# Sixteen modulation units beside the first two projection sections, K products in the ring slot, unit loads ahead of x, a maximum in the setup

## What is computed

```
mod = silu(c) @ w_ada + b_ada             # 9 rows (8 samples, 1 prompt) x 6144, in six parts
h = rms_norm(x, g_norm1) * (1 + sc1) + sh1
q, k, v, f, u, gate_b, gate_c = split(h @ w_in)        # one input projection
# samples: q over 4096 cached keys (paged), decay from cached log forgets, softmax, cached values
# prompt: causal attention of 512 tokens with a forget bias; short convolution beside it
x = x + ga1 * (concat(norm(attention), norm(convolution)) @ w_out)
x = x + ga2 * experts(rms_norm(x, g_norm2) * (1 + sc2) + sh2)   # 2 of 32 experts a token
y = rms_norm(x, g_final) * (1 + scf) + shf             # shf, scf = silu(c) @ w_ada_final + b
```

## Time and profile before

| | us |
|---|---|
| median of 3 runs | 970.69 (969.65 to 978.55) |
| the profiled execution | 973.92 |
| its span, first to last instruction | 972.2 |
| TensorE busy | 763.0 |
| VectorE busy | 499.3 |
| mean granted TensorE clock | 0.894 of full |
| moved by DMA | 319.28 MB, 328 GB/s on average |

### The profile page before, as it was taken

How to read it: one execution, slowest core, us unless ns; L and a number is a source line. 1 busy time by engine, 2 the same in 40 slices (tenths; PEclk the granted TensorE clock), 3 DMA queues, 4 the chain that set the end, 5 groups by cost and what they waited for, 6 DMA issues and landing times.

```text
span 972.2 us, 9885 instructions
## 1 busy us (share of the span) xinstructions
PE 763.0 (78%) x3822; PEld 350.9 (36%) x3822; DVE 499.3 (51%) x565; ACT 145.8 (15%) x333; POOL 276.0 (28%) x251
## 2 busy tenths in 40 slices
PE   5399977999998765658797799838888887778854
PEld 1044422333433211213353344434444444444421
DVE  1169979888999768684833232460111111111128
ACT  2221000201000122111142021201111111110103
POOL 4504435456643335251320000002222222212100
PEclk9689989999999877786799799858999999999967
DMA  8957669999999999999997900439999999999642
GB/s 319 400 195 260 217 216 363 420 417 416 418 422 359 364 387 413 398 420 422 377 369 257 351 22 22 173 132 354 411 411 413 412 410 412 412 412 412 273 190 88
DMA packets 67835, 319.28 MB, mean 328 GB/s; under 512 B 11436, under 2 KB 11464, under 8 KB 42567
## 3 DMA queue, kind: packets, MB, share of 16 engines
q1 hardware_dynamic: 41356, 166.53, 43.7%
q0 software_dynamic: 23936, 147.94, 38.3%
q10 hardware_dynamic: 2508, 4.35, 1.2%
HBM read 307.87 MB, written 15.05 MB: 332 GB/s over the span
## 4 chain that ended last, share of the span: by engine, by line
PE 32%; DMA 30%; DVE 24%; SPq 5%; issue 4%; ACT 2%; POOL 1%; DVEq 0%; POOLq 0%; ACTq 0%
DMA R_w<-in_w_expert_up_dram 10%; DVE R_x L1292 8%; DVE R_cm L1295 8%; PE banks L807 7%; DMA R_kv<-in_cache_v_dram,kv_index 6%; PE banks L683 6%; DMA R_kv<-in_cache_k_dram,kv_index 5%; PE banks L831 4%; DMA R_w<-in_w_in_dram 2%; DMA R_part<-in_cache_v_dram,kv_index 2%; PE banks L415 2%; DMA R_w<-in_w_ada_dram 2%; PE banks L823 1%; DMA R_q<-in_w_out_dram 1%; SPq L2013 1%
## 5 line engine op out<-in xcount | busy, mean ns | idle before, releaser
L1295 DVE TENSOR_REDUCE R_cm<-R_x 128x32 f32<-128x2048 f32 x64 | 146.3, 2286 | 7.0 <-DVE R_x L1292 0.5
L455 PE MATMUL banks<-R_h,R_w 128*128 128x512 f32 x320 | 144.8, 600 | 1.0 <-ACT R_h L956 1.0
L1292 DVE TENSOR_TENSOR R_x<-R_kv,R_part 128x2048 f32<-128x2048 f32 x44 | 100.7, 2288 | 15.0 <-DMA R_kv<-in_cache_k_dram,kv_index 14.1
L1856 POOL DMA_INDIRECT R_kv<-in_cache_k_dram,kv_index x44 | 64.1, 1457 | 151.9 <-DVE R_cm L1295 130.9
L415 PE MATMUL banks<-R_kv,R_cm 128*8 128x512 f32 x352 | 54.4, 698 | 47.9 <-DMA R_kv<-in_cache_v_dram,kv_index 41.4
L1913 POOL DMA_INDIRECT expert_rows_scratch<-R_h,R_part x32 | 32.0, 1001 | 204.8 <-DVE R_h L1720 204.8
L1856 POOL DMA_INDIRECT R_kv<-in_cache_v_dram,kv_index x44 | 70.6, 1604 | 67.3 <-PE banks L415 33.9
L455 PEld LDWEIGHTS banks<-R_h,R_w 128*128 128x128 f32 x320 | 58.7, 190 | 79.8 <-issue 78.6
L1717 DVE COPY R_h<-banks 128x128 f32<-128x128 f32 x32 | 9.3, 292 | 144.7 <-PE banks L823 144.7
L1910 POOL DMA_INDIRECT R_t<-h_scratch,R_part x32 | 31.3, 978 | 128.7 <-DVE R_part L1671 119.2
L1720 DVE TENSOR_SCALAR R_h<-banks,R_part 128x512 f32<-128x512 f32 x32 | 24.0, 751 | 71.6 <-PE banks L831 71.6
(11 more groups left out here) (329 smaller groups left out, 1234.2 us busy)
## 6 DMA issues: line engine op xcount, KB each, us to landing
R_w<-in_w_ada_dram SPq DMA_DIRECT2D x24, 1024.0 KB, 9.5
R_w<-in_w_in_dram SPq DMA_DIRECT2D x12, 1024.0 KB, 16.0
R_w<-in_w_ada_final_dram SPq DMA_DIRECT2D x8, 1024.0 KB, 10.3
R_kv<-in_w_expert_gate_dram SPq DMA_DIRECT2D x8, 1024.0 KB, 18.7
R_kv<-in_w_expert_up_dram SPq DMA_DIRECT2D x8, 1024.0 KB, 22.0
R_kv<-in_w_expert_down_dram SPq DMA_DIRECT2D x8, 1024.0 KB, 19.8
R_q<-in_w_expert_gate_dram SPq DMA_DIRECT2D x8, 1024.0 KB, 19.0
R_q<-in_w_expert_up_dram SPq DMA_DIRECT2D x8, 1024.0 KB, 22.8
```

The source lines that it names most:

```text
L455: last = nc.tensor.matmul(bank[m][:, :], l, r, start=(k == 0), stop=(k == KD - 1))
L1292: V.tensor_tensor(prod[:, :, :], kv_ring[slot][:, :, :], spread(q, [P, CH, HW]), ALU.mult)\
L1295: V.reduce_sum(scores[:, b, s * CH:(s + 1) * CH, :], prod[:, :, :].rearrange("p r (h d) -> p r h d", h=H), AX.X).then_inc(S["k_used"], 2)
L1856: pool.indirect_dma_start(kv_flat[slot], None, k_rows if kind == "k" else v_rows, bass.IndirectOffsetOnAxis(kv_index[:, n:n + 1], 0))\
```

## The change

Four pieces. (1) The 16 units of the second and third quarter of `w_ada` get two buffers of their own (`early_unit`: the place of `prod` in R_x, and a free part of R_cm) and are multiplied beside the 16 column groups of sections 0 and 1, into bank 5. ScalarE copies each quarter out, and VectorE's `modulation_early` runs at K chunk 24. Eight units of `w_ada_final` stay in the loop, in steps 1, 4, 7 and 10. (2) VectorE multiplies a K chunk in its ring slot, and the wait for the reduce before it is gone. (3) Units 8 and 9 are issued ahead of x; the gathers start when unit 9 has landed. (4) GpSimd takes a maximum over partitions of the constant ones at the end of its setup.

```diff
-        prod = view(R_x, 0, [CH, HW])
...
+        early_unit = [view(R_x, 0, [4 * SECS]), view(R_cm, 2088, [4 * SECS])]
...
-        ADA_AT = {w: n for n, w in enumerate((0, 1, 3, 4, 6, 8, 10, 12, 14, 16, 19, 22))}
+        ADA_AT = {w: n for n, w in enumerate((1, 4, 7, 10))}
...
+            def early_unit_product(i):
+
+                q, k = divmod(i, KD)
+                if i == 0:
+                    pe.wait_ge(S["f_taken"], 1)
+                if i == KD:
+                    pe.wait_ge(S["part_ready"], 2)
+                pe.wait_ge(early_loaded[i % 2], 16 * (i // 2 + 1))
+                for j in range(4):
+                    last = nc.tensor.matmul(bank[5][32 * j:32 * j + 32, :], c_t[:, k, :],
+                                            early_unit[i % 2][:, j * SECS:(j + 1) * SECS], start=(k == 0), stop=(k == KD - 1))
+                last.then_inc(S["early_used"], 1)
...
                 if c == 0:
                     pe.wait_ge(S["exp_ready"], b + 1)
+                    if b == 0:
+                        pe.wait_ge(S["part_ready"], 3)
...
             def beside_0(i):
+                early_unit_product(i)
...
             def beside_1(i):
+                early_unit_product(KD + i)
...
+            def early_evac(q):
+                act.wait_ge(S["early_used"], KD * (q + 1))
+                copy(part[q][:, :], bank[5][:, :]).then_inc(S["part_ready"], 1)
...
-            act.wait_ge(S["tail_done"], 1)
+            early_evac(0)
+            act.wait_ge(S["side_turned"], 2)
             copy(tail[:, :, :], bank[6][:, 64:64 + B * H].rearrange("p (b h) -> p b h", b=B))\
                 .then_inc(S["tail_evac"], 1)
...
                 if s == 1:
+                    early_evac(1)
                     soft_samples(0)
...
+            def modulation_early():
+
+                dve.wait_ge(S["part_ready"], 3)
+                dve.wait_ge(S["bands_loaded"], 16 * 10)
+                V.tensor_tensor(part[0][:, :], part[0][:, :], band[0][:, :], ALU.add).then_inc(S["mod_ready"], 1)
+                step(V.tensor_tensor(part[1][:, :], part[1][:, :], band[1][:, :], ALU.add))
+                V.scalar_tensor_tensor(part[1][0:64, :], part[1][0:64, :], 1.0, g_band[0][0:64, :], ALU.add, ALU.mult)\
+                    .then_inc(S["mod_ready"], 1)
...
-                if n:
-                    dve.wait_ge(S["k_used"], 2 * n)
-                V.tensor_tensor(prod[:, :, :], kv_ring[slot][:, :, :], spread(q, [P, CH, HW]), ALU.mult)\
-                    .then_inc(S["k_products"], 1)
+                chunk = kv_ring[slot][:, :, :]
+                V.tensor_tensor(chunk, chunk, spread(q, [P, CH, HW]), ALU.mult).then_inc(S["k_products"], 1)
                 dve.wait_ge(S["k_products"], n + 1)
                 V.reduce_sum(scores[:, b, s * CH:(s + 1) * CH, :],
-                             prod[:, :, :].rearrange("p r (h d) -> p r h d", h=H), AX.X).then_inc(S["k_used"], 2)
+                             kv_ring[slot].rearrange("p r (h d) -> p r h d", h=H), AX.X).then_inc(S["k_used"], 2)
...
+            forget_in(H, T, B, bank[5][0:H, 0:B], 1)
             for n in range(K_EARLY):
                 k_chunk(n)
-                if n == 0:
-                    forget_in(H, T, B, bank[5][0:H, 0:B], 1)
-                    V.memset(bank[5][:, :], 0.0)
+                if n == 24:
+                    modulation_early()
...
             def modulation():
 
                 dve.wait_ge(S["part_ready"], 4)
-                dve.wait_ge(S["bands_loaded"], 16 * 12)
-                V.tensor_tensor(part[0][:, :], part[0][:, :], bands[:, 0, :], ALU.add).then_inc(S["mod_ready"], 1)
...
+                dve.wait_ge(S["bands_loaded"], 16 * 16)
+                step(V.tensor_tensor(part[2][:, :], part[2][:, :], band[2][:, :], ALU.add))
...
+            G.partition_all_reduce(top_all[:, 0, :], ones[:, 0:H], P, RED.max)
...
-            pool.wait_ge(S["unit_used"], 8)
+            pool.wait_ge(unit_loaded[0], 16 * 4)
...
+            def early(i):
+
+                if i == 1:
+                    sp.wait_ge(S["h_psum"], 1 + KD)
+                if i >= 2:
+                    sp.wait_ge(S["early_used"], i - 1)
+                v, lo = quads[1 + i // KD]
+                sp.dma_start(early_unit[i % 2][:, :], v[:, i % KD, lo:lo + QUAD]).then_inc(early_loaded[i % 2], 16)
...
-            for u in range(8):
+            for u in range(10):
                 unit(u)
...
-            for u in range(8, 20):
+            for i in range(6):
+                early(i)
+            unit(11)
...
-            sp.wait_ge(S["unit_used"], 38)
+            sp.wait_ge(S["unit_used"], 14 + KD)
             for j in range(4):
...
+                bias_rows(j, 2)
```

More of the change, by code:

```diff
@@ L186, in build @@
         w_flat = view(R_w, 0, [3, 4 * SECS])
[L187 to L189 removed]
+        early_unit = [view(R_x, 0, [4 * SECS]), view(R_cm, 2088, [4 * SECS])]
+        part = [view(R_part, 1536, [SECS]), view(R_x, 1536, [SECS]), view(R_part, 5120, [SECS])]
+        band = [view(R_x, 0, [SECS]), view(R_x, SECS, [SECS]), view(R_w, 0, [SECS])]
+        g_band = [view(R_x, 2 * SECS, [SECS]), view(R_w, SECS, [SECS])]
         mix_a = view(R_h, 0, [C4, T + B])
@@ L269, in build @@
         unit_loaded = [sem(f"unit_loaded{i}") for i in range(3)]
+        early_loaded = [sem(f"early_loaded{i}") for i in range(2)]
         kv_loaded = [sem(f"kv_loaded{i}") for i in range(RING)]
@@ L1076, in conv_sqrt, with ada_evac @@
                 rsqrt(rt_c[:, 0:n], bank[6][:, 0:n], HD).then_inc(S["cn_sqrt"], 1)
-            def ada_evac(q):
-                act.wait_ge(S["unit_used"], 14 + KD * q)
-                if q == 3:
-                    act.wait_ge(S["qb_ready"], B)
-                copy(part[q - 1][:, :], bank[7][:, :]).then_inc(S["part_ready"], 1)
+            def ada_evac():
+                act.wait_ge(S["unit_used"], 14 + KD)
+                act.wait_ge(S["samp_t"], 3)
+                copy(part[2][:, :], bank[7][:, :]).then_inc(S["part_ready"], 1)
             def soft(u):
@@ L1992, in _ @@
             sp.dma_start(x_a[:, :, :], x_prompt.rearrange("b (t p) d -> (b p) t d", p=P)).then_inc(S["x_loaded"], 16)
+            unit(10)
             sp.dma_start(conv_sample[0, :, 0, :], state_conv[0, :, 1, :]).then_inc(S["outs"], 16)
-            for u in range(8, 20):
+            for i in range(6):
+                early(i)
+            unit(11)
+            sp.dma_start(state_rows[:, :], state_conv.rearrange("l b j c -> (l b j) c")).then_inc(S["wf_loaded"], 16)
+            for i in range(6, 10):
+                early(i)
@@ L1995, in _ @@
+            unit(12)
+            for i in range(10, 14):
+                early(i)
+            unit(13)
+            for i in range(14, 16):
+                early(i)
+            sp.wait_ge(S["early_used"], 2 * KD)
+            for j in range(4):
+                bias_rows(j, 0)
+                bias_rows(j, 1)
+            for j in range(2):
+                gain_rows(j, g_band[0], g_norm2)
+            for u in range(14, 18):
                 unit(u)
-                if u == 11:
-                    sp.wait_ge(S["h_row_ready"], 5)
-                    sp.dma_start(state_rows[:, :], state_conv.rearrange("l b j c -> (l b j) c")).then_inc(S["wf_loaded"], 16)
@@ L2012, in _ @@
+            for j in range(2, 4):
+                gain_rows(j, g_band[1], row(g_final))
             for lo, n, src in ((0, NG, w_router_group), (NG, NE, w_router_expert)):
@@ L2021, in _ @@
             sp.dma_start(wo[:, 6:KD, :], w_out_v[:, 6:KD, :]).then_inc(S["wo_conv_loaded"], 16)
-            for q in range(3):
-                sp.wait_ge(S["mod_ready"], q + 1)
-                for j in range(4):
-                    lo = (4 * q + j) * SECS
-                    sp.dma_start(mod_dram[:, lo:lo + SECS], part[q][32 * j:32 * j + B + 1, :]).then_inc(S["mod_out"], 16)
+            keep_modulation(2)
             sp.wait_ge(S["mod_out"], 16 * 12)
```

66 lines of the change are left out of this document (32 added, 34 removed).

## The result

| | us |
|---|---|
| before, median of 20 runs | 974.52 (968.42 to 978.55) |
| changed kernel, median of 20 runs | 966.96 (958.10 to 973.93) |
| ratio, with its 95% interval | 0.9925 (0.9904 to 0.9945), 7.3 us less |
| profiled executions, span | 972.2 before, 962.6 now |
| forecast | 22.7 us less |

The account below looks back on a forecast made before the run. DMA engines were taken as full from 182 to 300 and in the loop (328 to 481), with VectorE the bound there after the change. Terms +10 - 28 - 5 = -23 us, from 970.7 to 948; 8 in 10 for 924 to 970.

Parts of the forecast that it names:

- The start: Setup: unit 9 lands at about 32, x at 39.5; section 0 starts at 54.4, 6 us earlier (4 to 9).
- Sections 0 and 1: Input projection: 16 slots of 5.3 us, set by unit landings of 9.6; section 1 ends at 144.5 (131 to 164).
- the prediction's own signs of being wrong: Landings over 12 us with TensorE waiting, or granted clock below full, in sections 0 and 1; loop still near 145 us.
- The new waits: Around sections 0 to 2: VectorE waits 8 us for the tail sums' copy, ring stops at 153; both hidden.
- The attention loop: 20 K chunks: 153 us become 125 (109 to 142), VectorE's work plus half its waits, 28 us off.
- K products in the slot: VectorE's K products: no wait for the reduce before, 0.18 us a chunk, 3.6 us in the loop, inside the 125.
- The loop's end: Behind the attention loop: bias-row wait avoided, 4.1 us, and output weights issued sooner, 1 us; together 5 (4 to 7).
- C: Rival: the loop follows its score-to-product chain on a slowed TensorE; only 13 us come off, -8, 963; chance 0.18.
- B: Rival: DMA engines alone decide; 29 us gained, 34 to 40 with the loop's end and router rows, 932; chance 0.17.
- D: Rival: two buffers too few, units land in 14.6 us, the loop starts 50 us late, +17, 988; chance 0.12.
- No change: Whole kernel: time within 1% of before, the rest of C and a little of D; chance 0.18.

Follow-up runs that it names:

- e7: Kernel of e1 with the start as before: x ahead of units 8 and 9, gathers from the eighth used unit on; 950.92 us, ratio 0.9736.
- e1: Changed kernel with each V gather, from V chunk 28 on, one step earlier in the gathers' order; 942.63 us, ratio 0.9662.
- e5: Kernel before, with only the gathers' order of e1 (V a step ahead from chunk 28 on); 963.58 us, ratio 0.9891.
- e2: Changed kernel with the eight modulation units that stay in the loop loaded at a sixteenth of their width; 962.28 us, ratio 0.9857.
- e3: Changed kernel with the four router loads issued at the end, behind the last load of x, instead of mid-loop; 973.13 us, ratio 0.9991.

## Why the prediction was wrong

*The start* was right in kind. The gathers begin at 36.1, where unit 9 was to land at 32; x is there at 41.3 (39.5 was taken), and section 0 starts at 56.87 for 54.4. With the same start code the other runs put it between 52.7 and 61.0, and e7 leaves open how much of it is handed on.

*Sections 0 and 1* ended 4.8 us later than the likeliest value and well inside its bounds, 149.3 for 144.5; 2.5 of that is the later start. The length, 92.4 us for 90, is right in part by luck. The forecast had every slot last as long as half a unit's landing, 5.3 us. But where TensorE ran at full clock a column group and its unit product took 4.6 us, and at 14 of 16 products TensorE's row shows no wait. The rest was two waits, 3.29 and 4.26 us, and a clock below full behind them: eight matmuls of a section took 4.93 and 5.39 us there, elsewhere 3.70, and the granted clock was 0.97 from 60 to 122 and 0.88 from 122 to 150, one of the prediction's own signs of being wrong. The early units' loads, as issues of one line:

```profile
DMA to landing us min/median/max: 5.0/8.9/23.8
```

The Trainium skill's rule (DMA: Bandwidth & Descriptors, "Queues, rings and completion order"), that an engine takes the queues with work in turn, had put this end 5 to 7 us behind 144.5, for a gather queue that is never empty. By its own numbers (two units of 1.05 MB at half of 417 GB/s, 10.1 us and not 10.5) that is an estimated 4 us. The condition did not hold either: GpSimd issued no gather from 94.9 to 110.1, longer than the 10.7 us (median) in which K gathers into R_kv landed in this stage. So the 4.8 us neither bear the rule out nor speak against it.

*The new waits* were right. On its timeline VectorE stands 8.35 us behind the copy of the tail sums (8 forecast). It stops again at 155.8 (153 forecast), for 10.91 us, at the second maximum, whose turn on GpSimd comes behind V gathers that need V chunks 0 to 2:

```profile
102.01 0.63 DVE L1388 TENSOR_TENSOR R_t<-R_t 128x448 f32<-128x448 f32 x1 [8.35 <-ACT R_t L927]
...
166.67 0.17 DVE L1339 TENSOR_TENSOR R_t<-R_t 128x8 f32<-128x8 f32 x1 [10.91 <-POOL R_t L1888]
...
507.95 0.68 DVE L1543 TENSOR_TENSOR R_part<-R_part,R_w 128x512 f32<-128x512 f32 x1
```

Both are hidden, as said: V chunk 7 runs at 187.87 for 188, and the loop starts 9.6 us late for 10. That these two fit so well is luck in part: V chunk 0 came 4 us later than forecast, and from it to V chunk 7 section 2 then took 33.1 us, where 37 were forecast. The maximum of ones takes its idle time in the setup, ahead of the first gather:

```profile
22.04 0.39 POOL L1870 PARTITION_ALL_REDUCE R_t<-ones  x1 [8.08 <-issue]
```

*The attention loop* is the step that failed: "Between 109 (no wait left) and 142 (only the 7.0 and the 3.6 go) I take 125, its own work plus half of its waits". It took 139.1, next to the upper bound. The 18.0 us of waits for the attention output were put down to "late V chunks", and these to full DMA engines, so that half of the waits were to go with the bytes; only 3.6 of the 18.0 went. The V chunks were late by their landing and by their issue, behind a K gather that waits for VectorE. The change made the landings shorter (15.00 to 9.10 us for V chunk 39), but freeing bytes does not issue them sooner, and two units that it moved to the place behind V chunk 39 took back 3.6 us of it. Nothing in the rows of before told the two causes apart by itself, but the earlier trace rows have the release: a wait on TensorE's last product, whose V chunk can be followed back to its issue and to what released that, as the chain of before above shows. e1, which changes only the order of issue, takes these waits to 0.0, and e5 does so (18.0 to 0.2) in the kernel before. Two terms of the paragraph were misread besides. The 113.0 us of VectorE are busy time, which holds no waits, so the 3.6 could not be taken off: 112.6 were measured. And the waits for ScalarE's roots were 11.8 us, not 8.2.

*K products in the slot*: 0.18 us was right in size (0.19) and wrong in count, 4 places of 20, so 0.8 us and not 3.6. In the time it does not show. The Trainium skill's statement (VectorE: DVE Perf Modes, "The DRAIN you can't avoid") that a semaphore between chained instructions costs nothing extra differs from these rows, 2.40 against 2.20 us; the measurement decides.

*The loop's end* was right: VectorE's `modulation` no longer waits for bias rows (the third line of VectorE's timeline above), and the first output sum comes 5.7 us sooner behind the loop (5 forecast).

*The rivals.* C had the right size (loop -13, 8 us less in all), the right kind, a chain and not the bytes, and the right sign in the profile, the 18.0 us; the chain that it named, score to product on a TensorE below full clock, was not the one: e1 has the same steps at a granted clock of 0.76 and needs 120 us. B, bytes alone, falls by e2 and by a DMA share of 0.84 in the loop. D was told apart by its landings, a median of 8.9 us and not 14.6, though single ones were longer. No change is what the time came nearest to, at 0.75%, and that had been given 0.18.

## What to carry to other kernels

A wait that ends with a DMA is not yet a wait for bandwidth: follow the load back to its issue, and the issue to what released it, before a gain is worked out from bytes. Where two streams share one queue in a fixed order, each stream's slot waits hold up the other, and the consumer of one can come to wait for its own progress in the other; a step's lead in the order, alone, was here worth about as much (11 us) as the whole change, alone (7 us). And where two bounds lie close together, removing one shows little until the other goes as well, so try both before either is given up. Where an engine stands with no releaser in its row, look at the other engines' rows: in e3 it was a wait of VectorE, in whose fixed order the copy that TensorE needed came later. The best version here, the change with V gathers one step ahead, takes 0.966 to 0.971 of the time before.
